# First model's experts: the three extra chunk places hold the first half of every quad's weights, not of quad 1 alone

## What is computed

```python
def expert_block(args):
    xb, e = args
    h = jax.nn.silu(xb @ w_gate[e]) * (xb @ w_up[e])
    return h @ w_down[e]
...
contrib = ybuf[dest].astype(jnp.float32) * g_sorted[:, None]
y = jax.ops.segment_sum(contrib, tok_sorted, num_segments=T)
```

## Time and profile before

| | us |
|---|---|
| median of three runs | 2543.15 |
| profiled execution, own time | 2540.95 |
| its span | 2539.1 |
| first model's experts, layer 0 (first L1967 of quad 0 to the last `combine`) | 185.7 to 400.6 |
| first model's experts, layer 1 | to 801.2 |
| TensorE busy over the span | 2054.7 (81%) |
| GpSimd busy over the span | 76.6 (3%) |

### The profile page before, as it was taken

The page is one execution under the profiler, slowest core; times in us unless marked ns, Lnnn a source line. Parts: engine busy times, 40 slices in busy tenths (PEclk is TensorE's granted clock), DMA queues, the critical chain, the costliest instruction groups (busy, mean ns, idle before and its releaser), DMA issues. The chain is left out here.

```text
span 2539.1 us, 33840 instructions
## 1 busy us (share of the span) xinstructions
PE 2054.7 (81%) x14308; PEld 1302.4 (51%) x14309; DVE 637.7 (25%) x1483; ACT 376.2 (15%) x808; POOL 76.6 (3%) x104
## 2 busy tenths in 40 slices
PE   7898778898777999999966666689989998666665
PEld 5574336574334688888622222238888883222222
DVE  5452103551112236364200000022541121000001
ACT  1431001431002022200100000011211010000000
POOL 0201000101000000000000000000000000000000
PEclk9999989999888999999987888899999999888788
DMA  9359999355999332198899999973312369999996
GB/s 387 139 232 382 428 428 401 133 226 240 429 428 408 112 137 101 60 387 346 329 428 429 429 428 428 428 315 116 149 36 100 133 271 428 427 428 429 428 428 284
DMA packets 55842, 779.36 MB, mean 307 GB/s; under 512 B 6840, under 2 KB 7096, under 8 KB 8120
## 3 DMA queue, kind: packets, MB, share of 16 engines
q1 hardware_dynamic: 55736, 777.82, 73.6%
HBM read 776.75 MB, written 1.05 MB: 306 GB/s over the span
## 5 line engine op out<-in xcount | busy, mean ns | idle before, releaser
L1967 PE MATMUL bank<-ring,xnT 128*32 128x512 f32 x3136 | 480.4, 749 | 308.2 <-DMA ring<-in_w_exp 307.9
L1967 PEld LDWEIGHTS bank<-ring,xnT 128*32 128x32 f32 x3136 | 101.1, 124 | 675.0 <-DMA ring<-in_w_exp 356.3
L1992 PE MATMUL bank<-ring,arena 128*32 128x512 f32 x1440 | 174.2, 621 | 73.1 <-DMA ring<-in_w_exp 38.8
L971 PE MATMUL bank<-xnT,ring 128*128 128x256 f32 x960 | 210.7, 379 | 0.0
L2163 DVE TENSOR_TENSOR arena<-bank,arena 128x256 f32<-128x256 f32 (+1 forms) x33 | 18.3, 553 | 718.3 <-PE bank L1967 517.4
L971 PEld LDWEIGHTS bank<-xnT,ring 128*128 128x128 f32 x960 | 181.6, 190 | 28.4 <-issue 4.5
L1657 PE MATMUL bank<-xnT,ring 128*128 128x256 f32 x768 | 173.6, 379 | 0.0
L1657 PEld LDWEIGHTS bank<-xnT,ring 128*128 128x128 f32 x768 | 146.1, 190 | 22.1 <-issue 2.5
L1926 PE MATMUL bank<-arena,xnT 128*128 128x256 f32 x592 | 144.5, 399 | 3.6 <-DVE xnT L2174 3.6
L1926 PEld LDWEIGHTS bank<-arena,xnT 128*128 128x128 f32 x592 | 114.7, 199 | 62.8 <-issue 47.8
L1992 PEld LDWEIGHTS bank<-ring,arena 128*32 128x32 f32 x1440 | 48.3, 112 | 174.7 <-issue 72.5
(11 more groups left out here) (435 smaller groups left out, 2050.0 us busy)
## 6 DMA issues: line engine op xcount, KB each, us to landing
ring<-in_w_exp SPq DMA_DIRECT2D x274, 2048.0 KB, 25.7
arena<-in_w_ada SPq DMA_DIRECT2D x24, 2048.0 KB, 11.6
ring<-in_w_in SPq DMA_DIRECT2D x20, 2048.0 KB, 25.9
ring<-in_w_merge SPq DMA_DIRECT2D x18, 2048.0 KB, 8.2
arena<-in_w_exp SPq DMA_DIRECT2D x14, 2048.0 KB, 15.0
ring<-in_w_o SPq DMA_DIRECT2D x8, 2048.0 KB, 11.7
ring<-in_w_conv SPq DMA_DIRECT2D x6, 2048.0 KB, 8.0
ring<-in_w_rest SPq DMA_DIRECT2D x2, 1696.0 KB, 25.5
```

Of the source, the lines that this page charges most:

```text
L971: last = nc.tensor.matmul(o[:, T * j:T * j + T], w[:, k, col:col + P], xnT[:, k, :], start=k == 0, stop=k == KT - 1)
L1967: last = nc.tensor.matmul(o[rows(e), :], Xw[:, k, rows(e)], w[:, at:at + MW], start=k == 0, stop=k == KT - 1)
L1992: last = nc.tensor.matmul(o[rows(e), :], hidT[:, j, rows(e)], w[:, at:at + MW], start=j == 0, stop=j == ft - 1)
```

## The change

SP fetches (q,3), (q,4), (q,5) into the ring for every quad from 1 to 7. Behind these three, for q up to 6, it issues the loads of (q+1,0), (q+1,1), (q+1,2) into the extra places; each of them first waits until the place's chunk of quad q has been copied into the ring. GpSimd now runs its three copies for each of the quads 1 to 7; before each three it waits until all three loads have landed (the count is 48 a quad).

```diff
-                            for n in range(EXTRA1 if q == 1 else 0, RING):
+                            for n in range(EXTRA1, RING):
                                 sp.wait_ge(w_used(), last_item + (n0 + n + 1))
                                 fetch(q, n)
+                            for n in range(EXTRA1 if q + 1 < NQ else 0):
+                                sp.wait_ge(w_loaded(slot(n)), 16 * ((r0 + n) // RING + 1) + 16 * q)
+                                sp.dma_start(extra[spots[n]], feed(q + 1, n)).then_inc(extra_in, 16)
...
-                        last_item = pool.value_load(offs[0:1, LAST_AT:LAST_AT + 1], min_val=0, max_val=ITEMS * per_turn)
-                        for n in range(EXTRA1):
-                            pool.wait_ge(extra_in, 16 * extras)
-                            pool.wait_ge(w_used(), last_item + (n0 + n + 1))
-                            nc.gpsimd.tensor_copy(ring[:, place(r0 + n), :], extra[spots[n]]).then_inc(w_loaded(slot(n)), 16)
+                        for q in range(1, NQ):
+                            last_item = pool.value_load(offs[0:1, LAST_AT + q - 1:LAST_AT + q], min_val=0, max_val=ITEMS * per_turn)
+                            pool.wait_ge(extra_in, 16 * extras * q)
+                            for n in range(EXTRA1):
+                                pool.wait_ge(w_used(), last_item + (n0 + n + 1))
+                                nc.gpsimd.tensor_copy(ring[:, place(r0 + n), :], extra[spots[n]]).then_inc(w_loaded(slot(n)), 16)
```

## The result

The changed kernel is slower by half a per cent: a median of 2558.26 us over 8 runs (2550.32 to 2561.84) against 2542.69 us (2539.39 to 2551.29), ratio 1.0051 with a 95% interval of 1.0034 to 1.0069, which is +13.0 us (8.6 to 17.5). (The ratio is estimated from all runs and isn't the quotient of the two medians, which lie 15.6 us apart.) The forecast was 2557, between 2551 and 2565. The profiled execution has a span of 2548.3 us, 9.2 more than before, and lies at the lower end of the runs.

The account below looks back on a forecast made before the run. DMA landings were taken to bound the kernel, so only quad 7's copies delay: 6.5 + 6.5 = 13.0 us, plus 0.2 and 0.8, 14.0 over 2540.95 is 2554.95; median set at 2557, range 2551 to 2565.

Parts of the forecast that it names:

- slack: Quads 2 to 7: loads still issued early enough to keep the DMA queue full, with at least 5.9 us to spare.
- the tail: Behind quad 7's chunk 2 landing, three serial copies and two chunks delay each layer's stage by 6.5 us.
- the wait of down's second chunk: Layer 1, quad 7: an earlier load wait of 1.34 us hides part of 8.0 us, leaving 6.5 us delay.
- two unknown terms: Way from copy's end to TensorE, +0.1 us a layer, and slow TensorE clock, 0.8 us in the two layers.
- the slow clock: Quad 7's chunks 2 and 3: one chunk in the two layers runs at half TensorE clock, 0.8 us.
- VectorE against GpSimd: Lock-out between VectorE instructions and GpSimd's copies: up to 3.6 us where on the path, counted as 0.
- Slow clock all through: Rival, 10%: TensorE stays at half clock in chunks 2 and 3 of both layers, about 20 us, 2563.
- Queue dry: Rival, 6%: longer copies or a thinner queue use up the slack and six quads pay; 2569, up to 2590.
- Hidden delay: Rival, 6%: the next stage hangs on loads landing at unchanged times, so the 6.5 us vanish; 2543.
- Faster: Rival, 4%: front holes filled and copies paced one by one by landings; tail costs 0, some 5 us won, 2538.
- the hole at 200 us: Layer 0's front, 200 to 205 us: DMA idle about 2.7 us; the forecast took the change's gain there as 0.
- the one at 580 us: Layer 1's front, 580 to 585 us: DMA idle 5 us in quad 0's second item; gain taken as 0.

Follow-up runs that it names:

- last quad direct: Changed kernel with copies for quads 1 to 6 only; quad 7's six chunks go straight into the ring. Ratio 0.9994 against the kernel before, stages -1.6 us.
- only the last quad by copies: Changed kernel with copies for quads 1 and 7 alone, quads 2 to 6 loaded straight into the ring. Ratio 1.0042 against the kernel before, stages +12.2 us.
- early refill: Changed kernel with extra places for quads 1 and 2 only; SP issues (2,0) to (2,2) right behind (1,3). Ratio 0.9970 against the kernel before.
- early refill with all quads: Changed kernel with (2,0) to (2,2) issued ahead of (1,4) and (1,5), each copy waiting for its own load. Ratio 0.9979 against the kernel before.

## Why the prediction was right

**What bounds the stage** was read rightly. The landings are the clock: in the changed kernel, too, the queue is full at 1.01, and the issue times came within 0.5 us of the prediction's list. The slack it worked out (5.9 us) held, and was overdrawn when the copies were made twice.

**The delay is the tail's alone.** Shown from both sides: last quad direct (nothing left), only the last quad by copies (all of it). The last combine of layer 0 started at 402.74; the prediction said 403.6. (The near match is flattered by 0.5 us, since this execution began the stage later; from the stage's start the combine came 1.4 us earlier than forecast.)

**The sum, term by term, layer 0** (from the stage's start at 185.66 and 186.17):

| | predicted, us | measured, us |
|---|---|---|
| landing of quad 7's chunk 2 | unchanged | 193.90 to 192.94, -1.0 |
| three copies | 10.8 | 10.69 |
| from the last copy's end to TensorE | +0.1 over before | 389.80 to 389.95, 0.15 |
| chunks 2 and 3 | 3.84, some slow | 3.57, both at full clock |
| same stretch before, 379.56 to 387.68 | 8.12 | |
| delay at the middle of the item | 6.5 | 5.3 |

In layer 1 the delay at the middle was 6.8 us (8.0 forecast), and the wait of down's second chunk hid 1.5 of it, as the prediction had worked out.

The stage as a whole was 5.15 us longer in layer 0 and 5.24 in layer 1, where 6.5 + 6.5 was forecast, 14.0 us in all with the two unknown terms. So the mechanism was right and the sum 3.6 us too large. Three sizes were off, all to one side: the loads came a little quicker (1.0 us a layer), two full-clock chunks in a row took 3.57 us and not twice 1.92 (0.3 a layer), and the slow clock, 0.8 us, did not come: TensorE had left half clock by the time chunk 2 was copied. The stretches of the changed kernel show it:

```profile
377.00:383.00 6.00, 0.23 (x4) 0.20 (x8) 0.59 (x1) 0.00 (x0) 3.89 (x2) 0.73 1.02 437
383.00:390.00 7.00, 5.39 (x36) 0.92 (x32) 0.00 (x0) 0.00 (x0) 6.80 (x2) 0.74 1.00 428
390.00:394.00 4.00, 4.00 (x34) 1.50 (x35) 0.00 (x0) 0.35 (x1) 0.00 (x0) 1.00 1.02 430
```

Half-clock time falls to chunks 0 and 1, which have room behind the next copy. So what the traces hold is +10, and the runs' +13 (8.6 to 17.5) and +9.9 (6.4 to 13.5) agree with it. The forecast of +14.0 lies inside the first interval and just above the second. That the median of 2558.26 came within 1.3 us of 2557 is partly luck: the scatter of that median stood in for what the sum had too much.

**VectorE against GpSimd.** The one-hot (L2078 now) in layer 0 of the changed kernel, for the earlier trace rows, first the stretch of quad 1's copies, then the rest:

```profile
L2078 DVE TENSOR_TENSOR arena<-cst,arena x1: 3198/3198/3198, 194.2 to 194.2; 128x256 f32<-128x256 f32 x1
```

```profile
L2078 DVE TENSOR_TENSOR arena<-cst,arena x6: 424/426/427, 208.1 to 349.1; 128x256 f32<-128x256 f32 x6
```

Only the one-hot that was caught before is caught now; six more ran beside no copy, as forecast. The lock-out that the Trainium skill ("SBUF — State Buffer", SBUF: two separate sides) states agrees with the 3198 ns: the one-hot ended 0.3 us behind the end of the first copy. The instruction behind it on this path, the weighted form, met the third copy (1.98 us in place of 0.42; 1.97 in the kernel before). Both cost no more than before: TensorE waited 0.53 us for the one-hot, 0.49 before.

**The rivals.** Slow clock all through: none of the 12 pairs of chunks 2 and 3 (six quads a layer) was slow in the changed kernel. Queue dry: did not happen, and happens at 7.3 us a copy. Hidden delay: L453 moved with the stage. Faster: both of its conditions were right as conditions. The copies paced one by one take the tail away, and the early refill fills the hole at 200 us. In layer 1 the prediction named the wrong hole: the one at 580 us lies in the first item of quad 0 and nothing here fills it, the one that the refill fills comes 20 us later. The kernel as changed fills none of them.

## What to carry to other kernels

Where loads set the pace and their queue stays full, a stage costs its last landing plus what stands behind it: a step added between landing and use is free in every round but the last, and there it costs in full. A wait for a group of loads puts the work on all of them behind the last one; give each load its own semaphore, and work that is shorter than the distance of two landings (here 3.60 against 4.84 us) hides in it. More buffer is worth only the idle time of the queue that it can reach in the issue order, so look for the hole first and put the refill ahead of the waits that make it.

## What the runs showed of the hardware

**Loads by the extra places come quicker.** A quad's six chunks land every 29.20 us where three of them go into the extra places (431 GB/s), and every 29.35 to 29.38 us where all go into the ring (428). That held in each kernel of either kind, with short copies as with full ones, with a full queue and a thin one, and with the ring moved. It is 0.6%, 1 us a layer. The landings one by one say where it sits: with the queue full a load into an extra place lands 4.84 us behind the one ahead (median), a load into the ring 4.89 us, side by side in the same quad, in every trace that has both. In the kernel with the last quad direct the period goes back from 29.21 to 29.37 us with quad 7, and where only the last quad goes by copies it falls from 29.38 to 29.21. So it hangs on the destination of the single load. Why one destination is quicker stays open.

**TensorE's clock in a part that nothing touched.** From the norm at the start of the second model's layer 1 to the experts of that layer the traces fall into three lengths: 421 us, 424.5 us and 428 us. The difference goes with the clock. Stretches that begin 225 us behind the norm, of early refill with all quads (428 us), then of the kernel before (421 us):

```profile
1885.00:1910.00 25.00, 21.61 (x473) 19.21 (x457) 7.08 (x17) 2.46 (x3) 0.00 (x0) 0.70 0.01 3
```

```profile
1894.00:1919.00 25.00, 21.72 (x518) 18.84 (x509) 8.61 (x18) 3.99 (x6) 0.00 (x0) 1.00 0.01 4
```

The granted clock is 0.70 in one and 1.00 in the other, with TensorE as busy (21.6 and 21.7 us of 25). It sorts all twelve traces: 1.00 in the five of 421 us, 0.86 in the three of 424.5, 0.69 or 0.70 in the four of 428. A shift of earlier work by some us may decide which of the three an execution meets; no run tells. It is as large as the effect under study, so effects of this size were read in the stages of the traces first, and in the whole time second.
